# A TensorE filler behind the score segments of the first three units of a dilated attention

## The reference

```python
DIL_CONFIGS = ((128, 1), (512, 4), (2048, 16))
DIL_HEADS_PER_GROUP = 4
...
        for g, (w, dil) in enumerate(DIL_CONFIGS):
            steps = np.arange(w // dil + 1) * dil
...
            s = (jnp.einsum('bhqd,bhqnd->bhqn', qblk[:, g], kg).astype(jnp.float32) * scale
                 - slopes[g][:, None, None] * steps_f[None, None, :])
            valid = (qpos[:, None] - jnp.asarray(steps)[None, :]) >= 0
            s = jnp.where(valid, s, -jnp.inf)
            m = jnp.max(s, axis=-1, keepdims=True)
            e = jnp.exp(s - m)
            den = jnp.sum(e, axis=-1, keepdims=True)
            o = jnp.einsum('bhqn,bhqnd->bhqd', (e / den).astype(v.dtype), vg)
            outs.append(o.astype(jnp.float32))
            lses.append((m + jnp.log(den))[..., 0])
        wts = jax.nn.softmax(jnp.stack(lses, axis=0), axis=0)
        o = jnp.einsum('gbhq,gbhqd->bhqd', wts, jnp.stack(outs, axis=0))
```

## Time and profile before

| | |
|---|---|
| median of 3 executions | 1998.24 us (1997.92 to 1999.78) |
| the profiled execution | 1997.92 us |
| its span, first to last instruction | 1996.1 us |
| mean granted TensorE clock | 0.995 |
| TensorE matmuls busy | 1939.1 us (97%) |
| VectorE busy | 919.2 us (46%) |
| ScalarE busy | 713.5 us (36%) |
| GpSimd (POOL) busy | 22.6 us (1%) |
| DMA, mean | 174 GB/s |
| instructions | 23836 |

### The profile page before, as it was taken

How to read it: one execution, slowest core, us unless ns; L and a number is a source line. 1 busy time by engine, 2 the same in 40 slices (tenths; PEclk the granted TensorE clock), 3 DMA queues, 4 the chain that set the end, 5 groups by cost and what they waited for, 6 DMA issues and landing times.

```text
span 1996.1 us, 23836 instructions
## 1 busy us (share of the span) xinstructions
PE 1939.1 (97%) x9831; PEld 1332.0 (67%) x9831; DVE 919.2 (46%) x1487; ACT 713.5 (36%) x1185; POOL 22.6 (1%) x33
## 2 busy tenths in 40 slices
PE   6999999999999899999999999999999999999999
PEld 4756643333333267777788887877787778888787
DVE  4375412222111145475376665335555456666533
ACT  4365211111111141575343333235343643333323
POOL 1000000000000000000000000000000000000000
PEclk9999999999999999999999999999999999999999
DMA  9677479999999951401143323221212023332311
GB/s 324 147 283 223 197 295 427 428 428 427 427 427 427 426 155 32 148 1 43 43 119 93 103 87 103 88 85 64 84 64 64 22 64 106 85 106 85 106 64 42
DMA packets 168038, 346.43 MB, mean 174 GB/s; under 512 B 19643, under 2 KB 142267, under 8 KB 152443
## 3 DMA queue, kind: packets, MB, share of 16 engines
q1 hardware_dynamic: 165907, 340.85, 46.7%
q10 hardware_dynamic: 1224, 2.15, 0.9%
q0 software_dynamic: 800, 1.91, 0.4%
HBM read 340.70 MB, written 4.19 MB: 173 GB/s over the span
## 4 chain that ended last, share of the span: by engine, by line
PE 88%; DMA 7%; DVE 3%; ACT 2%; issue 1%; SPq 0%; DVEq 0%
PE bank L2158 22%; PE bank L1389 13%; PE bank L2175 12%; PE bank L1972 10%; PE bank L1991 4%; PE bank L1339 2%; PE bank L903 2%; PE bank L923 2%; DMA norm_area<-in_w_down 2%; DMA moe_high<-in_w_up 2%; PE bank L944 2%; DMA work<-in_w_up 2%; PE bank L1327 2%; PE bank L1941 1%; DMA ring<-in_w_ada 1%; PE bank L2003 1%
## 5 line engine op out<-in xcount | busy, mean ns | idle before, releaser
L561 DVE TENSOR_TENSOR ring_low<-ring,w_high 128x2048 fp32r<-128x2048 f32 (+1 forms) x91 | 207.7, 2282 | 122.6 <-ACT w_high L551 122.5
L2158 PE MATMUL bank<-h_high,ring_low 128*128 128x512 f32 x640 | 249.7, 390 | 0.0
L551 ACT ACTIVATE w_high<-ring 128x2048 fp32r<-128x2048 f32 x90 | 171.3, 1905 | 218.5 <-PE bank L2158 174.0
L2158 PE MATMUL bank<-low_ff,w_high 128*128 128x512 f32 x608 | 238.3, 392 | 0.0
L2158 PE MATMUL bank<-h_high,w_high 128*128 128x512 f32 x608 | 236.5, 389 | 0.0
L2175 PE MATMUL bank<-ff_split,w_high 128*128 128x512 f32 x704 | 222.4, 396 | 1.6 <-DVE work L2874 1.6
L2175 PEld LDWEIGHTS bank<-ff_split,w_high 128*128 128x128 f32 x704 | 132.3, 188 | 35.8 <-DVE work L2874 2.4
L2175 PE MATMUL bank<-ff_split,ring_low 128*128 128x512 f32 x352 | 139.2, 396 | 0.0
L2158 PEld LDWEIGHTS bank<-h_high,ring_low 128*128 128x128 f32 x640 | 120.3, 188 | 26.5
L2158 PEld LDWEIGHTS bank<-h_high,w_high 128*128 128x128 f32 x608 | 114.1, 188 | 25.2
L2158 PEld LDWEIGHTS bank<-low_ff,w_high 128*128 128x128 f32 x608 | 114.1, 188 | 24.5
(11 more groups left out here) (462 smaller groups left out, 3375.3 us busy)
## 6 DMA issues: line engine op xcount, KB each, us to landing
ring<-in_ffn_w_up SPq DMA_DIRECT2D x88, 512.0 KB, 5.2
ring<-in_w_gate SPq DMA_DIRECT2D x16, 2048.0 KB, 22.7
ring<-in_w_down SPq DMA_DIRECT2D x12, 2048.0 KB, 26.9
ring<-in_ffn_w_down SPq DMA_DIRECT2D x22, 1024.0 KB, 4.9
ring<-in_w_ada SPq DMA_DIRECT2D x18, 1024.0 KB, 7.7
const<-in_w_gate SPq DMA_DIRECT2D x8, 2048.0 KB, 22.7
work<-in_w_up SPq DMA_DIRECT2D x8, 2048.0 KB, 22.6
ring<-in_w_up SPq DMA_DIRECT2D x8, 2048.0 KB, 23.2
```

Source lines behind the costliest of these rows:

```text
L551: act.activation(high_of(n, words), slab_view(g)[:, 0:words], ACT.Copy).then_inc(sem("split_high"), 1)
L561: dve.tensor_tensor(ring_low[:, slot_of(g), 0:words], slab_view(g)[:, 0:words], high_of(n, words).bitcast(F32), ALU.subtract).then_inc(sem ...
L2158: mm = pe.matmul(bank[n % 6][:, :], st[k], mv[k], start=(k == 0), stop=(k == len(st) - 1))
```

## The change

Behind each score segment of a unit below `filled`, one call of the filler is put into TensorE's program, into the unit's bank of the values: bank 6 for units 0 and 2, bank 7 for unit 1. Only the dilated attention is called with `filled=3`, so there are nine calls. They have no wait and set no semaphore, and nothing reads what they write. The other attentions keep `filled=0` and are the same as before.

```diff
-        def attention_pe(pe, att, after_scores=None, before_last=None, steps=None):
+        def attention_pe(pe, att, after_scores=None, before_last=None, steps=None, filled=0):
...
                         for r, (_, _, (bias, b0)) in enumerate(seg):
                             mm = pe.matmul(o[r][:, b0:w], ident_r, bias, start=False, stop=True)
                     mm.then_inc(sem("att_scores"), 1)
+                    if u < filled:
+                        keep_busy(pe, att.out_banks[u % len(att.out_banks)], 1)
...
-            attention_pe(pe, DIL_A, before_last=out3_begun)
+            attention_pe(pe, DIL_A, before_last=out3_begun, filled=3)
```

## The result

| | before | after |
|---|---|---|
| median of 10 executions | 1998.38 us (1996.98 to 2002.35) | 2003.42 us (2002.57 to 2004.76) |
| ratio to before | | 1.0023, 95% interval 1.0015 to 1.0031 |
| profiled execution | 1997.92 us | 2003.92 us |
| its span | 1996.1 us | 2002.1 us |
| mean granted clock | 0.995 | 0.993 |

The change costs 5.0 us (2003.42 - 1998.38), by the interval 3.0 to 6.2 us. The forecast was 3.5, of the right sign and too small. 2003.42 lies at the very edge of the stated range, which ended at 2003.4. It is 0.9 us above the range that the forecast had for itself (2000.8 to 2002.5), and beyond the 0.2% border of 2002.24, to which the prediction gave 0.37; the interval of the ratio, 1.0015 to 1.0031, has that border inside.

What follows compares the result with a forecast made beforehand. The prediction took TensorE to bound the changed stage: its pieces summed to 15.99 us against 12.27, 3.7 us more, which on the profiled 1997.92 gave 2001.6, taken as 2001.7 us; range 1999.3 to 2003.4.

Steps and rivals of the forecast that it cites:

- TensorE becomes the bound of the stage: From unit 0's first scores to unit 3's in the dilated attention, TensorE never waits: 15.99 us against 12.27.
- The price of a filler: In the changed stage: seven fillers before scores at 0.95 us each, two before transposes at 0.86, 6.65 and 1.72 us.
- such a late load: Behind a change of shape in the stage, a weight load coming late: 0.06 us in the transposes, some 0.10 in the bounds.
- The walk of the waits: Stage waits on VectorE and ScalarE: TensorE waits for nobody from 1525.07 to 1541.1 us; unit 2's exponents start near 1540.6.
- The shift goes through to the end: From unit 3's scores to the end of the kernel, everything comes 3.7 us later.
- The clock: Unit 0's eight transposes in the stage run at full instead of half clock, paying back 1.07 us.
- rivals 1 and 4: Clock still falls in the stage, 2003.3 us, chance 0.13; later half-clock stretch comes or goes, 2003.4 or 2000.0, chance 0.10.
- the first (clock falls all the same): In the changed stage the clock still falls for 3.4 us, 1.7 us more: 2003.3 us, chance 0.13.
- The second (cheaper fillers): In the changed stage weight loads hide or filler records overlap with 64-row score segments: 1999.2 us, chance 0.14.
- The third (faster): In the changed stage the clock pays back more than the fillers take: 1997.2 us, chance 0.03.
- The fourth: In a later stage another half-clock stretch comes or goes, 1.7 us either way: 2000.0 or 2003.4 us, chance 0.10.

## Why the prediction was right, and where its size was off

**TensorE becomes the bound of the stage**: shown. There is no idle time from 1526.5 to 1543.4 us, the stage repeats to the hundredth, and the runs with other fillers came out as sums with the prices measured by then had said: 13.33 for half the columns (13.1 to 13.4 expected), 14.05 without the switch (14.1), 11.96 for unit 2 (12.0).

**The price of a filler** is the term that was mis-sized. The sum took seven at 0.95 and two at 0.86 us; they measured 1.055, between 1.05 and 1.06, and 0.96. The missing 0.10 is within the filler: its first record holds the engine for 0.53 us before the second starts, not 0.43. The forecast took the step from six fillers in a row, whose shape does not change. Rows of weight loads show what differs: among the six of before, between products of 128 rows, the first load starts 0.10 us ahead of the first record (1606.83 against 1606.93); behind 64-row scores it starts with it (both 1526.89); the 64-row filler's is 0.22 ahead (1536.12 against 1536.34). In this order:

```profile
1606.83 0.30 PEld L1224 LDWEIGHTS bank<-const 128*128 128x128 f32 x2
1526.89 0.30 PEld L1226 LDWEIGHTS bank<-const 128*128 128x128 f32 x2
1536.12 0.40 PEld L912 LDWEIGHTS bank<-const 64*128 64x128 f32 x2
```

The forecast had such a late load for scores and for transposes, where rows of before show it, and put it at nothing for the filler, without a row. Some 0.105 for each of nine is 0.95 us, and 15.99 + 0.95 = 16.94 is the measured stage. Scores and transposes were priced right to 0.01 us.

**The walk of the waits** held: TensorE reached unit 1's transposes 1.27 us after ScalarE's copies had freed the banks (1541.17), where the walk had some 1.1. Its times for the exponents of units 1 and 2 were 0.4 and 0.8 us too early, measured from the start of the stage, because the fillers take longer. **The shift goes through to the end**: shown; the rest is 458.7 to 458.8 us in all four profiles of before and both of after.

**The clock** was right in the changed kernel and mis-stated for before. The forecast counted 1.1 us of regained clock as certain, since its one profile had it. Three of four profiles of before did not. Set against the 11.40 us of those, the loss is 5.5 us; with one in four at 12.27 it is 5.3. The medians say 5.0, and their interval holds all of these. So two terms were short by 0.9 us each, both to the same side. That the time still came out at the end of the stated range, and not clearly beyond it, is luck: this end was set by rivals 1 and 4, and neither of them happened. The profiled execution's own 2003.92 was 6.0 over the first one of before, of which 1.4 is the early clock.

Of the rivals, the first (clock falls all the same) did not occur in two profiles of the changed kernel. The reason given against it, that the fillers remove the idle time ahead of the fall, is weaker than it looked: three of four profiles of before have the idle time and no fall. The second (cheaper fillers) is refuted in this shape, but is what a 64-row filler partly does. The third (faster) fails by the same sums: even the one filler that costs nothing shows no gain that 11 executions could tell. The fourth put a half-clock stretch into a later stage. None came: the rest is the same in both kernels. Such stretches come and go ahead of the stage, in both, and move its start between 1525.1 and 1527.2 us over all runs here.

The Trainium skill, "TensorE: Matmul & The Clock Gate", section "Back-to-back issue gap", gave 216 ns for one isolated matmul of 512 columns. The trace after disagrees for this fp32 product, with 0.43 and 0.53 us for a record; the rows of before had 0.43.

What stays open: whether a filler in the idle time of unit 2 keeps the clock up at all. It would take many profiles, since the loss was there in one of four, and was worth 0.9 us then. Open as well: that the 0.10 within the filler is its first weight load is read from the starts of the load rows; no run changes the load alone.

## What to carry to other kernels

A filler is free only in time in which its engine would have stood idle; what it takes beyond that lands on the path, and when it stands ahead of the idle time it delays the engines that are fed and can leave the idle time as it was. Price it with the change of shape on both sides and its own weight load, from a place where the neighbours have other shapes. Before a change is made for a half-clock stretch, look whether it is there in more than one profile.

## What the runs showed of the hardware

- A 128-row fp32 matmul of 512 columns steps by 0.43 us behind its like and by 0.53 us as the first behind 64-row products; with 64 rows it stepped by 0.43 there. The filler's first weight load started with its product behind 64-row scores, 0.10 us ahead of it behind 128-row products, and 0.22 us ahead where the filler had 64 rows.
- The same program lost the clock in this stage in one profile of four, with the same 1.5 us of idle TensorE in all four. With fillers in unit 0 alone it fell in two of two.
- Nine fillers of 16 columns did not keep the clock from falling, in the one profile taken.
